# Windowed attention core of a hybrid diffusion trunk: the mask of item w goes ahead of the denominators of item w-1 on VectorE, and GpSimd multiplies the probabilities by the reciprocal of their sum

## What is computed

```
def attend_block(qb, keys, values, masks, sink):
    scale = HEAD_DIM ** -0.5
    scores = []
    for kp, mk in zip(keys, masks):
        s = einsum('bqkgd,bskd->bkgqs', qb, kp) * scale
        if mk is not None:
            s = where(mk, s, NEG_INF)
        scores.append(s)
    m = sink_f
    for s in scores:
        m = maximum(m, max(s, axis=-1))
    denom = exp(sink_f - m)
    for s, vp in zip(scores, values):
        p = exp(s - m[..., None])
        denom = denom + sum(p, axis=-1)
        out = out + einsum('bkgqs,bskd->bqkgd', p, vp)
    return out / denom
```

## Time and profile before

| | us |
|---|---|
| median of 3 runs | 2988.97 (2988.23 to 2990.68) |
| span of the profiled execution | 2988.2 |
| TensorE busy | 2801.6 (94%) |
| VectorE busy | 1607.8 (54%) |
| ScalarE busy | 1184.5 (40%) |
| GpSimd busy | 109.7 (4%) |
| attention core of layer 0, first mask to last h_lo | 190.7 to 343.0 |
| attention core of layer 3 | 2291.1 to 2444 |

### The profile page before, as it was taken

How to read it: one execution, slowest core, us unless ns; L and a number is a source line. 1 busy time by engine, 2 the same in 40 slices (tenths; PEclk the granted TensorE clock), 3 DMA queues, 4 the chain that set the end, 5 groups by cost and what they waited for, 6 DMA issues and landing times.

```text
span 2988.2 us, 51513 instructions
## 1 busy us (share of the span) xinstructions
PE 2801.6 (94%) x19936; PEld 2645.5 (89%) x19936; DVE 1607.8 (54%) x2878; ACT 1184.5 (40%) x2042; POOL 109.7 (4%) x71
## 2 busy tenths in 40 slices
PE   5977799999998999999989999999998779999999
PEld 4965699999998999999969999999997569999999
DVE  2667556625644664366342665366367754663662
ACT  2347445414423552243232543244234754541441
POOL 1000010000002000000201000000100001000000
PEclk7989899999999999999989999999998989999999
DMA  6410133323320332333201332333121002221222
GB/s 233 181 64 1 50 125 134 137 74 135 136 93 33 138 134 103 123 133 130 66 24 57 120 134 100 111 134 127 63 78 36 1 15 61 78 84 64 73 85 74
DMA packets 62431, 279.67 MB, mean 94 GB/s; under 512 B 7392, under 2 KB 9568, under 8 KB 49632
## 3 DMA queue, kind: packets, MB, share of 16 engines
q1 hardware_dynamic: 62304, 277.93, 27.0%
HBM read 274.74 MB, written 3.16 MB: 93 GB/s over the span
## 4 chain that ended last, share of the span: by engine, by line
PE 86%; DVE 6%; ACT 6%; issue 2%; DMA 1%; SPq 0%; POOL 0%; DVEq 0%; ACTq 0%
PE ps L457 73%; ACT prob L923 3%; PE ps L541 3%; PE ps L480 3%; PE ps L743 1%; PE ps L552 1%; DVE prob L1265 1%; DVE prob L1282 1%; PE ps L502 1%; DMA ada_w<-in_ada_w 1%; ACT stat L925 1%; PE ps L680 1%; PE ps L649 1%; PE ps L510 1%; PE ps L635 1%
## 5 line engine op out<-in xcount | busy, mean ns | idle before, releaser
L457 PE MATMUL ps<-h_hi,w_hi 128*128 128x322 f32 x3392 | 799.8, 317 | 7.2 <-DVE w_lo L1057 4.1
L457 PE MATMUL ps<-h_lo,w_hi 128*128 128x322 f32 x3392 | 784.8, 313 | 0.0
L457 PE MATMUL ps<-h_hi,w_lo 128*128 128x322 f32 x3392 | 780.6, 312 | 0.0
L803 ACT ACTIVATE w_hi<-w_raw 128x1024 fp32r<-128x1024 f32 (+1 forms) x288 | 325.5, 1130 | 1037.1 <-PE ps L457 921.1
L457 PEld LDWEIGHTS ps<-h_hi,w_hi 128*128 128x128 f32 x3392 | 569.6, 190 | 34.0 <-issue 28.4
L457 PEld LDWEIGHTS ps<-h_lo,w_hi 128*128 128x128 f32 x3392 | 577.4, 190 | 0.0
L457 PEld LDWEIGHTS ps<-h_hi,w_lo 128*128 128x128 f32 x3392 | 577.0, 190 | 0.0
L1057 DVE TENSOR_TENSOR w_lo<-w_raw,w_hi 128x1024 fp32r<-128x1024 f32 (+1 forms) x288 | 377.3, 1310 | 67.6 <-ACT w_hi L803 65.9
L1177 DVE SCALAR_TENSOR_TENSOR x<-ps,mods,x 128x321 f32<-128x321 f32 (+5 forms) x264 | 99.9, 435 | 537.1 <-PE ps L457 537.1
L457 PE MATMUL ps<-f_hi,w_hi 128*128 128x322 f32 x1408 | 325.1, 312 | 0.0
L457 PE MATMUL ps<-f_hi,w_lo 128*128 128x322 f32 x1408 | 324.5, 312 | 0.0
(11 more groups left out here) (119 smaller groups left out, 2533.1 us busy)
## 6 DMA issues: line engine op xcount, KB each, us to landing
ada_w<-in_ada_w SPq DMA_DIRECT2D x96, 1024.0 KB, 5.5
w_raw<-in_w_in SPq DMA_DIRECT2D x176, 512.0 KB, 3.6
w_raw<-in_w_out SPq DMA_DIRECT2D x64, 704.0 KB, 4.0
w_raw<-in_w_qkv SPq DMA_DIRECT2D x24, 512.0 KB, 5.1
w_raw<-in_w_o SPq DMA_DIRECT2D x16, 512.0 KB, 3.8
w_raw<-in_w_fnet SPq DMA_DIRECT2D x8, 512.0 KB, 3.6
x<-in_x SPq DMA_DIRECT2D x1, 2576.0 KB, 15.5
out_y<-x SPq DMA_DIRECT2D x8, 322.0 KB, 3.7
```

The source lines that it names most:

```text
L457: mm = pe.matmul(ps[:, 2 * par + hf, 0:NH], w[par][:, kk, :], b[:, hf * NH:(hf + 1) * NH], start=(kk == 0 and n == 0), stop=(kk == k - 1 a ...
L803: act.activation(w_hi[par][:, 0:k, :], w_raw[par][:, 0:k, :], ACT.Copy).then_inc(hi_made, 1)
```

## The change

VectorE's loop calls `masked(w)` ahead of `normed(w-1)`. `normed` keeps the addition and the reciprocal and now signals `inv_denom`; the two multiplies of an item become two GpSimd instructions with the same operands, in place, which signal `p_ready`. TensorE, ScalarE and SyncE have the same instructions with the same waits.

```diff
@@ gpsimd
                         pool.tensor_tensor(sq_sum[:], sq_sum[:], sq[kk % 2][:], ALU.add).then_inc(sq_added, 1)
+                    if KINDS[layer] == "attn" and not second:
+                        w0 = 40 * (layer // 3)
+                        for w in range(w0, w0 + 40):
+                            nb, _ = WORK[w - w0]
+                            lo, hi = KEYS[nb]
+                            hi = 512 if nb < 4 else hi
+                            pool.wait_ge(inv_denom, w + 1)
+                            for hd in range(2):
+                                pool.tensor_scalar(prob[w % 2][hd][:, lo:hi], prob[w % 2][hd][:, lo:hi],
+                                                   stat[:, w % 2, hd, 5:6], None, ALU.mult).then_inc(p_ready, 1)
@@ vector, attention core
                     def normed(w):
-                        nb, _ = WORK[w - w0]
-                        lo, hi = KEYS[nb]
-                        hi = 512 if nb < 4 else hi
                         dve.wait_ge(exp_made, 2 * w + 2)
                         st = stat[:, w % 2, :, :]
                         own.link(dve.tensor_tensor(st[:, :, 4:5], st[:, :, 2:3], st[:, :, 3:4], ALU.add))
-                        own.link(dve.reciprocal(st[:, :, 5:6], st[:, :, 4:5]))
-                        for hd in range(2):
-                            dve.tensor_scalar(prob[w % 2][hd][:, lo:hi], prob[w % 2][hd][:, lo:hi],
-                                              st[:, hd, 5:6], None, ALU.mult).then_inc(p_ready, 1)
+                        dve.reciprocal(st[:, :, 5:6], st[:, :, 4:5]).then_inc(inv_denom, 1)
...
                     for w in range(w0, w0 + 43):
+                        if w < w0 + 40:
+                            masked(w)
                         if 1 <= w - w0 <= 40:
                             normed(w - 1)
-                        if w < w0 + 40:
-                            masked(w)
                         if w - w0 >= 3:
                             out_lo(w - 3)
```

## The result

| | us |
|---|---|
| before, median of 4 runs | 2989.16 |
| after, median of 4 runs | 3257.65 (3255.21 to 3259.51) |
| ratio, 95% interval | 1.0895 (1.0880 to 1.0911) |
| forecast | 3057.6, range 3014 to 3135 |

The change makes the kernel 9% slower. The sign was forecast, and so was the loop that causes it; the size was not: the loss is 268 us where 69 were forecast, and the time lies outside the range.

What follows compares the result with a forecast made beforehand. It took the serial VectorE and ScalarE softmax loop, 4.10 us a 512-column item, as the bound. The new loop, 3.50 us plus two 0.77 us multiplies, added 34.3 us a layer, 68.6 in two, giving 3057.6 us; range 3014 to 3135.

Steps and rivals of the forecast that it cites:

- that is again a loop of one item, with two engines more in it: Attention softmax: masks, sums, GpSimd multiplies, transposes and scores form a one-item loop, 5.04 us at 512 columns against 4.10.
- faster: Rival: masks run beside exponentials in the attention softmax, turn 3.2 us for 4.10, kernel 2929 us; chance 0.03.
- the walk: One round of the new softmax loop at 512 columns, full clock: 3.50 us plus two GpSimd multiplies.
- three handoffs: VectorE to GpSimd, GpSimd to TensorE, TensorE to VectorE in the new loop: estimated 0.1 us each, 0.30 in all.
- lower clock: Rival: TensorE stays at the lower clock throughout the attention cores, doubling its terms, kernel 3106 us; chance 0.18.
- half of the add's price per column, since it reads half as much: Price of one GpSimd softmax multiply: 0.11 us plus 1.28 ns a column, 0.77 us at 512 columns.
- the upper bound: Most one GpSimd softmax multiply could cost, at the two-input add's 2.56 ns a column: 1.42 us at 512 columns.
- the second head's lie beside the first mask: TensorE's scores in the new loop: only the first head's count, 0.57 of 1.14 us at 512 columns.
- Blocks 1 and 2 stay at full clock in this sum: Attention blocks 1 and 2: TensorE's 3.17 us of work an item is 63% of 5.04, so full clock holds.
- if the turn is 3.50 plus twice something else, only X was: Check on the softmax turn after: such a turn would mean only X, the GpSimd multiply's price of 0.77 us, was wrong.
- Dear multiply: Rival: GpSimd's softmax multiply costs 1.42 us at 512 columns, kernel 3141 us, about 3190 with lower clock; chance 0.11.
- in each other's way: Rival: VectorE and GpSimd contend in the attention cores, multiplies slowed by a factor of 1.36, kernel 3094 us; chance 0.03.

Runs made afterwards that it cites:

- the first two experiments: Against the kernel before: masks ahead of sums on VectorE, which still multiplies, 3051.25 us (1.0210); then old order with multiplies on GpSimd, 2991.80 us (1.0005).
- three buffers and moved scores: Changed kernel (GpSimd multiplies) with three probability buffers and TensorE's order scores of w+1, values of w-2, transposes of w-1: 2944.76 us, 0.9851 of before.
- idle time filled: Changed kernel with extra identity matmuls on TensorE ahead of each wait for a head's multiply: 3174.76 us, 1.0617 of before.
- scores ahead: Changed kernel with TensorE issuing the scores of w+1 ahead of the transposes of w-1: 3116.02 us, 1.0422 of before.

## Why the prediction was wrong

**The loop was right.** The step "that is again a loop of one item, with two engines more in it" is shown by the chain of the changed kernel, by the first two experiments (order alone 2.1%, multiply alone nothing) and by the ones that break it. That exponentials leave the chain, and that masks wait for the scores, was right too. So was the reason against the rival "faster": the program order, not the price, decides; with three buffers and moved scores the same multiply is a gain.

**Its terms were too small.** For a 512-column item, the walk against the two chains:

| term | walk | measured | where |
|---|---|---|---|
| two masks | 1.72 | 1.72 | after |
| sum, reciprocal and the three handoffs | 0.70 | 0.56 | after |
| two multiplies | 1.54 | 3.12 | after |
| second head's transposes | 0.51 | 0.66 | idle time filled |
| scores | 0.57 | 1.13 | idle time filled |
| lower clock | 0 | 1.40 | 8.59 - 7.19 |
| turn | 5.04 | 8.59 | |

- *The multiply*, "half of the add's price per column, since it reads half as much". This is the largest error: 0.79 us an instruction at 512 columns, 0.64 at 384 and 0.33 at 128, 2 x (0.79 x 24 + 0.64 x 8 + 0.33 x 8) = 53 us a layer and 107 in all. The same step set the upper bound, by the argument that an instruction with one input can't cost more than one with two, and this bound did not hold either (1.56 against 1.42): the column price is the same (2.5 and 2.56 ns), and the fixed part is 0.28 us where the fill's 0.11 had been put. The Trainium skill, "GPSIMD Engine Reference", section 4.1, calls one-input work roughly line-rate; the measurement, 2.5 ns a column where the fill takes 0.82, does not agree and decides.
- *The scores*, "the second head's lie beside the first mask". They do not; both heads' scores are in the loop. 0.56 us for 16 items, 0.46 for 16, 0.40 for 8: 20 us a layer, 39 in all. The experiment with scores ahead settled it. The trace of before already had the two heads in pairs: its last two L623 start at 256.20, 0.01 us apart, and both are done 0.28 us later.
- *The clock*, "Blocks 1 and 2 stay at full clock in this sum", taken at a chance of four in five. It fell for a part of the time in all blocks, and the filled version puts 83 us on it, of which the sum had 14 in block 3 and about 6 in block 4. The step was worked out from a turn of 5.04 us, of which 3.17 us of work at full clock are 63%. The turn is 8.59 us, and the same work is 37% of it (an estimate from the earlier trace rows). The window of the changed kernel has 63% too, 20.30 of 32 us, but at a granted clock of 0.66, where the scores take 2.08 us and not 1.13; that the two figures agree is chance. Nor did the step hold near its own turn. The kernel with VectorE's order alone has a turn of 4.95 us, and there the clock is not 1.00 either:

```profile
256.00:288.00 32.00, 22.28 (x206) 16.77 (x204) 18.66 (x67) 18.98 (x55) 0.00 (x0) 0.93 0.01 2
```


The three are 107 + 39 + 63 = 209 us against the 200 between 3057.6 and 3257.65. Two smaller errors nearly cancel: the handoffs were put 0.14 us an item too high (11 us in all) and the transposes 0.15 us too low at 512 columns (about 10 us in all). What is left, about 8 us, is not divided further; the second mask of each core, which starts only 1.44 us after the first, belongs to it.

So the size was wrong by three steps, and the prediction's own sign for it, "if the turn is 3.50 plus twice something else, only X was", says the same: with the measured multiply that would be 6.62 us, and the turn is 8.59.

**The rivals.** Dear multiply and lower clock came true together, a case that the prediction worked out at 3190 and left outside its range. Even that is 68 us short; the second head's scores are 39 of them and the 0.14 to 0.16 us by which the multiply exceeds its bound are 23. It took the two as separate chances, though here they come together: the long turn leaves TensorE idle, and filling that idle time brings the clock back. VectorE and GpSimd were not in each other's way. In the changed kernel no mask runs beside a multiply, so it can't show this; in the kernel with the multiply on GpSimd only, 48 masks of 512 columns lie wholly inside a multiply and take 0.69 us as elsewhere, and the multiply keeps its 1.56 us.

## What to carry to other kernels

When an instruction is moved ahead on an in-order engine, list what it waits for and ask what stands behind it: a loop of one item pays every member in every item, while in a loop that goes round two items it pays half of them. An operation that is dear on its engine may cost nothing or everything; whether it lies in the shortest loop decides, and here moving the scores, a buffer and the mask together gave 2.5% where the mask alone lost 2.1%. If an engine has never run an instruction of that form in the trace, the upper bound is not the nearest relative's price but something above it, and the clock's fall belongs in the same scenario as the longer turn. When two instructions of TensorE use different halves of the partitions, look at a narrow window of the trace before putting half of their time on the first.

## What the runs showed of the hardware

- A float32 multiply of one SBUF input on GpSimd takes 0.28 us and 2.5 ns a column (602, 1244 and 1564 ns at 128, 384 and 512 columns), the column price of a two-input add; a constant in place of a per-partition operand saves 75 ns. VectorE does the pair of 512 columns in 0.88 us, GpSimd in 3.12.
- The granted clock of the stretch 256 to 288 is 1.00 before, 0.93 with VectorE's new order alone (turn 4.95 us), 0.84 in the changed kernel with scores ahead (6.02) and 0.66 in the changed kernel (8.59). With useless matmuls in the idle time, TensorE busy for 25.67 of 32 us, it is 1.00, and the kernel 83 us faster.
- The score matmuls of two heads, which lie on different halves of the partitions (64 each), run beside each other: they start in pairs 0.01 us apart (two of L631 within 1.02 us, two of L634 within 0.43), and the heads are signalled 0.06 us apart.
- A mask on VectorE (one input in PSUM, one in SBUF) takes 0.69 us inside a GpSimd multiply as outside, and the multiply takes 1.56 us with it or without.
